# Turning the normalized head results by VectorE's 32x32 blocks and scratch memory instead of by TensorE, in heads 0 to 6 of both kinds

## The reference, cut to what matters

```
def rms_norm(x, g):
    y = xf * lax.rsqrt(jnp.mean(jnp.square(xf), axis=-1, keepdims=True) + RMS_EPS) * g
fo = rms_norm(fo, fox_norm_w_l).reshape(bsz, t_, FOX_WIDTH)      # 8 fox heads
o = rms_norm(o, norm_w) * jax.nn.silu(z)                         # 8 GDN heads
out = jnp.concatenate([fo, go], axis=-1) @ w_out_l               # output projection
```

## Time and profile before

| | us |
|---|---|
| median of 3 runs | 1889.69 (1888.07 to 1890.96) |
| the profiled execution | 1889.48 |
| its span, first to last instruction | 1887.9 |
| granted TensorE clock, mean | 0.997 of full speed |
| fox heads | about 90 to 310 us, one every 30 us |
| GDN heads | about 310 to 700 us, one every 48 us |

### The profile page before, as it was taken

One profiled execution on the slowest core, in us unless ns is written; L12 is line 12 of the kernel. 1 busy time (PEld: TensorE's weight loads), 2 busy tenths in 40 slices (PEclk: granted clock), 3 DMA queues, 4 the chain that ended last, 5 costly groups with the idle time before them and its releaser, 6 DMA issues.

```text
span 1887.9 us, 31205 instructions
## 1 busy us (share of the span) xinstructions
PE 1861.8 (99%) x9409; PEld 1577.3 (84%) x9409; DVE 1076.7 (57%) x2353; ACT 729.3 (39%) x1467; POOL 268.5 (14%) x491
## 2 busy tenths in 40 slices
PE   7999999999999999999999999999999999999997
PEld 6999998888888888888888888888888888888886
DVE  6666666888888874664545454433334444444455
ACT  4444344554555433343333333333333333333330
POOL 2343433333333310001111110000000000000000
PEclk9999999999999999999999999999999999999999
DMA  7666674444444335245556645544445555467441
GB/s 209 184 162 160 164 172 124 117 112 112 116 112 117 117 114 164 91 129 165 156 152 165 173 128 164 162 130 129 129 129 146 145 164 162 122 167 212 162 134 67
DMA packets 317413, 270.77 MB, mean 143 GB/s; under 512 B 96600, under 2 KB 230624, under 8 KB 316704
## 3 DMA queue, kind: packets, MB, share of 16 engines
q1 hardware_dynamic: 306880, 250.90, 47.4%
q0 software_dynamic: 10464, 18.99, 4.0%
HBM read 249.73 MB, written 20.06 MB: 143 GB/s over the span
## 4 chain that ended last, share of the span: by engine, by line
PE 97%; DVE 1%; DMA 1%; SPq 1%; issue 0%; ACT 0%; DVEq 0%; POOL 0%; ACTq 0%; POOLq 0%
PE bank L298 70%; PE bank L2033 9%; PE bank L1769 7%; PE bank L1885 2%; PE bank L1245 1%; PE bank L1227 1%; PE bank L1239 1%; PE bank L1221 1%; SPq L230 1%; DMA x_res<-in_x_sample 0%; PE bank L1195 0%; DMA raw<-in_w_in 0%; PE bank L640 0%; PE bank L1288 0%; PE bank L417 0%
## 5 line engine op out<-in xcount | busy, mean ns | idle before, releaser
L274 DVE TENSOR_TENSOR w_lo<-raw,w_hi 128x512 fp32r<-128x512 f32 (+2 forms) x828 | 565.3, 691 | 620.4 <-ACT w_hi L269 617.2
L269 ACT ACTIVATE w_hi<-raw 128x512 fp32r<-128x512 f32 (+2 forms) x828 | 502.6, 616 | 838.2 <-PE bank L298 700.8
L298 PE MATMUL bank<-w_hi,aT_hi 128*128 128x512 f32 (+2 forms) x1776 | 695.7, 392 | 2.0 <-DVE aT_lo L432 1.6
L298 PE MATMUL bank<-w_hi,aT_lo 128*128 128x512 f32 (+2 forms) x1776 | 673.2, 379 | 0.0
L298 PE MATMUL bank<-w_lo,aT_hi 128*128 128x512 f32 (+2 forms) x1776 | 672.1, 378 | 0.0
L298 PEld LDWEIGHTS bank<-w_hi,aT_hi 128*128 128x128 f32 x1776 | 334.4, 188 | 60.3 <-issue 9.4
L298 PEld LDWEIGHTS bank<-w_hi,aT_lo 128*128 128x128 f32 x1776 | 333.7, 188 | 55.4
L298 PEld LDWEIGHTS bank<-w_lo,aT_hi 128*128 128x128 f32 x1776 | 334.7, 188 | 47.4
L298 PE MATMUL bank<-w_hi,hT_hi 128*128 128x512 f32 x288 | 112.0, 389 | 0.0
L298 PE MATMUL bank<-w_lo,hT_hi 128*128 128x512 f32 x288 | 112.0, 389 | 0.0
L298 PE MATMUL bank<-w_hi,hT_lo 128*128 128x512 f32 x288 | 112.0, 389 | 0.0
(11 more groups left out here) (366 smaller groups left out, 1986.8 us busy)
## 6 DMA issues: line engine op xcount, KB each, us to landing
raw<-in_ffn_w_gate SPq DMA_DIRECT2D x176, 256.0 KB, 2.7
raw<-in_ffn_w_up SPq DMA_DIRECT2D x176, 256.0 KB, 2.7
raw<-in_ffn_w_down SPq DMA_DIRECT2D x176, 256.0 KB, 3.3
raw<-in_w_in SPq DMA_DIRECT2D x128, 192.0 KB, 2.4
raw<-in_w_in SPq DMA_DIRECT2D x128, 128.0 KB, 2.3
raw<-in_w_in SPq DMA_DIRECT2D x256, 64.0 KB, 2.3
raw<-in_w_out SPq DMA_DIRECT2D x61, 256.0 KB, 3.2
h_blocks<-sg SPq DMA_DIRECT2D x11, 768.0 KB, 4.5
```

The source lines that it names most:

```text
L269: nc.scalar.activation(w_hi[:, g % RING, 0:width], raw[:, g % RAW, 0:width], ACT.Copy).then_inc(sem("w_high"), 1)
L274: nc.vector.tensor_tensor(w_lo[:, g % RING, 0:width], raw[:, g % RAW, 0:width], w_hi[:, g % RING, 0:width], ALU.subtract).then_inc(sem("w_ ...
L298: last = nc.tensor.matmul(acc[t][:, 0:width], l[:, k0 + n, t * P:(t + 1) * P], r[:, g % RING, 0:width], start=(n == 0 and j == 0), stop=(n ...
```

## The change

In heads 0 to 6 of both kinds TensorE no longer turns the normalized result. VectorE transposes its 32x32 blocks in one instruction over all three tiles (128x384), to `sc` in fox heads and `R` in GDN heads, and waits for its own last write first. SyncE stores the 192 KB to the scratch tensor `turns`, waits for the store, and loads them back in four DMAs that put the blocks in place, in runs of 32 elements, to `pT` (fox) and `vn` (GDN). ScalarE's high part and VectorE's low part are computed from there in the next head: in fox heads at slot 8 on ScalarE and before the mask additions on VectorE, in GDN heads at slot 14 on both. In the last head of each kind everything stays with TensorE. The results of GDN head h now lie in place h + 1 (mod 8) of `mixG`; head 0 writes place 0 first with values that the last head overwrites.

On SyncE the fox store stands before piece 9 and the load before piece 11; in GDN heads the store stands before piece 11 and the load before piece 14, behind the load of the next states.

```diff
+TURN_STORE_AT, TURN_LOAD_AT, TURN_MIX_AT = 9, 11, 8
...
+            turns = nc.dram_tensor("turns", (TOK, HD), F32, kind="Internal").ap()
+
+            def turned_by_pe(h):
+
+                return isinstance(h, int) and h == HEADS - 1
+
+            def store_turned(sp, tile, ready, count):
+                sp.wait_ge(sem(ready), count)
+                sp.dma_start(turns.rearrange("(t p) f -> p t f", p=P), tile).then_inc(sem("o_stored"), 16)
+
+            def load_moved(sp, tile, h):
+                sp.wait_ge(sem("o_stored"), 16 * (h + 1))
+                for r in range(4):
+                    sp.dma_start(
+                        tile[SQUARE * r:SQUARE * (r + 1), :].rearrange("b (a c) -> b a c", c=SQUARE),
+                        turns.rearrange("(a b) (r c) -> b r a c", b=SQUARE, r=4)[:, r]).then_inc(sem("o_moved"), 16)
...
+                fturn = sc[:].rearrange("p t c -> p (t c)")[:, 0:TOK]
+                fmoved = pT[:].rearrange("p t c -> p (t c)")[:, 0:TOK]
...
-                    yield 41 + min(later, FIRST_TURN_LATER)
-                    W("f_o")
-                    for t in range(TT):
-                        last = nc.tensor.transpose(b3[:, t * P:(t + 1) * P], fo[:, t, :], ident)
-                    last.then_inc(sem("f_oT_ps"), 1)
-                    yield 45 + later
-                    W("f_mix")
+                    if turned_by_pe(h):
+                        yield 41
+                        W("f_o")
+                        for t in range(TT):
+                            last = nc.tensor.transpose(b3[:, t * P:(t + 1) * P], fo[:, t, :], ident)
+                        last.then_inc(sem("f_oT_ps"), 1)
+                        yield 45
+                        W("f_mix")
...
+                    else:
+                        yield TURN_MIX_AT
+                        act.wait_ge(sem("o_moved"), 64 * h)
+                        nc.scalar.activation(mixF_hi[:, bass.ds(h - 1, 1), :], fmoved.unsqueeze(1), ACT.Copy,
+                                             scale=nwf[:]).then_inc(sem("f_mix_hi"), 1)
...
+                        dve.wait_ge(sem("f_mix_hi"), h)
+                        nc.vector.scalar_tensor_tensor(
+                            out=mixF_lo[:, bass.ds(h - 1, 1), :], in0=fmoved.unsqueeze(1), scalar=nwf[:],
+                            in1=mixF_hi[:, bass.ds(h - 1, 1), :], op0=ALU.mult, op1=ALU.subtract)\
+                            .then_inc(sem("f_mix"), 1)
...
+                    if not turned_by_pe(h):
+                        after(last)
+                        nc.vector.transpose(fturn, fo[:].rearrange("p t c -> p (t c)"))\
+                            .then_inc(sem("f_o"), 1)
+                        assert own[0] == F_OWN
+                        return
+                    own[0] += 1
                     last.then_inc(sem("f_o"), 1)
...
+                    def next_turn(n, h):
+                        if n == TURN_STORE_AT:
+                            store_turned(sp, fturn.rearrange("p (t c) -> p t c", t=TT), "f_o", h + 1)
+                        if n == TURN_LOAD_AT:
+                            load_moved(sp, fmoved, h)
                     with sp.Fori(0, HEADS - 2) as i:
                         for n in range(NP_IN):
+                            next_turn(n, i)
                             loads(sp, 2 * NP_IN + n + NP_IN * i, n % RAW, fox_parts(i + 2, n, n % RAW))
...
-                        if p == 2:
-                            W("g_mix")
...
-                    yield LEVELS_DONE + 10
-                    W("g_o")
-                    for t in range(TT):
-                        last = nc.tensor.transpose(tl(turn_bank(h), t), go[:, t, :], ident)
-                    last.then_inc(sem("g_oT_ps"), 1)
+                    if last_head(h):
+                        yield LEVELS_DONE + 10
+                        W("g_o")
+                        for t in range(TT):
+                            last = nc.tensor.transpose(tl(turn_bank(h), t), go[:, t, :], ident)
+                        last.then_inc(sem("g_oT_ps"), 1)
...
+                    yield 14
+                    act.wait_ge(sem("o_moved"), 64 * (HEADS - 1 + h))
+                    nc.scalar.activation(mixG_hi[:, bass.ds(h, 1), :], vn.rearrange("p t c -> p (t c)").unsqueeze(1),
+                                         ACT.Copy, scale=nwg2[:]).then_inc(sem("g_mix_hi"), 1)
...
+                        if n == 1:
+                            W("g_mix_hi")
+                            V.scalar_tensor_tensor(out=mixG_lo[:, bass.ds(h, 1), :],
+                                                   in0=vn.rearrange("p t c -> p (t c)").unsqueeze(1), scalar=nwg2[:],
+                                                   in1=mixG_hi[:, bass.ds(h, 1), :], op0=ALU.mult,
+                                                   op1=ALU.subtract).then_inc(sem("g_mix"), 1)
...
+                    if last_head(h):
+                        own[0] += 1
+                        ins.then_inc(sem("g_o"), 1)
+                    else:
+                        after(ins)
+                        V.transpose(R.rearrange("p t c -> p (t c)"), go[:].rearrange("p t c -> p (t c)"))\
+                            .then_inc(sem("g_o"), 1)
...
+                    if n == STORE_AT - 1:
+                        store_turned(eng, R, "g_o", h + 1)
                     if n == STORE_AT:
                         store_state(eng, h)
                     if n == STORE_AT + 2:
                         eng.wait_ge(sem("g_S_out"), 32 * (h + 1))
                         load_state(eng, h + 1)
+                        load_moved(eng, vn.rearrange("p t c -> p (t c)"), HEADS - 1 + h)
...
-                    dve.sem_inc(sem("g_mix"), 1)
...
-                            last = nc.tensor.matmul(banks[t][:, :], l[:, k % HEADS, t * P:(t + 1) * P], r,
+                            last = nc.tensor.matmul(banks[t][:, :], l[:, k if k < HEADS else (k + 1) % HEADS,
+                                                                      t * P:(t + 1) * P], r,
```

More of the change, by code:

```diff
@@ L104 @@
 SAMPLE_LEVELS = 4
-F_OWN = 14
+F_OWN = 15
 ROWS = 2 * 3 * 8 + 8 * 8
@@ L109 @@
 WARM_IN = 20
-G_OWN = 25
+G_OWN = 26
 G_READ = 15
@@ L898, in fox_act @@
                     nc.scalar.activation(pT[:, 0:4, :], tiles(b6[:, :], 4), ACT.Copy).then_inc(sem("f_pT0"), 1)
-                    yield 41 + min(later, FIRST_TURN_LATER)
-                    W("f_oT_ps")
+                    if not turned_by_pe(h):
+                        return
+                    yield 41
+                    act.wait_ge(sem("f_oT_ps"), 1)
                     nc.scalar.activation(mixF_hi[:, bass.ds(h, 1), :], b3[:, 0:TOK].unsqueeze(1), ACT.Copy, scale=nwf[:])\
@@ L1197, in gdn_pe @@
                     yield 9
-                    L("g_cv", 1, 3), W("g_mix")
+                    L("g_cv", 1, 3)
                     for t in range(TT):
@@ L1387, in gdn_act @@
                     decays(range(5, NB)).then_inc(sem("g_Sdec"), 1)
[L1388 to L1391 removed]
+                    if last_head(h):
+                        yield 48
+                        act.wait_ge(sem("g_oT_ps"), 1)
+                        nc.scalar.activation(mixG_hi[:, bass.ds((h + 1) % HEADS, 1), :], turn_bank(h)[:, 0:TOK].unsqueeze(1),
+                                             ACT.Copy, scale=nwg2[:]).then_inc(sem("g_mix_hi"), 1)
                 def gdn_dve(dve, h):
@@ L1430, in gdn_dve @@
                     dve.wait_ge(sem("g_rows_in"), 16 * (h + 1))
+                    W("g_state")
                     for t in range(TT):
@@ L1550, in gdn_dve @@
                     ins.then_inc(sem("g_state"), 1)
-                    yield 48
-                    W("g_mix_hi")
-                    V.scalar_tensor_tensor(out=mixG_lo[:, bass.ds(h, 1), :], in0=turn_bank(h)[:, 0:TOK].unsqueeze(1),
-                                           scalar=nwg2[:], in1=mixG_hi[:, bass.ds(h, 1), :], op0=ALU.mult,
-                                           op1=ALU.subtract).then_inc(sem("g_mix"), 1)
+                    if last_head(h):
+                        yield 48
+                        dve.wait_ge(sem("g_mix_hi"), h + 2)
+                        V.scalar_tensor_tensor(out=mixG_lo[:, bass.ds((h + 1) % HEADS, 1), :],
+                                               in0=turn_bank(h)[:, 0:TOK].unsqueeze(1), scalar=nwg2[:],
+                                               in1=mixG_hi[:, bass.ds((h + 1) % HEADS, 1), :], op0=ALU.mult,
+                                               op1=ALU.subtract).then_inc(sem("g_mix"), 1)
                     assert own[0] == G_OWN
```

7 lines of the change are left out of this document (2 added, 5 removed).

## The result

The changed kernel takes 1933.74 us (median of four runs, 1928.26 to 1934.76) against 1889.82 for the kernel before beside it: a ratio of 1.0228 (95% interval 1.0215 to 1.0241), 44 us slower. Forecast were 1920 us and the range 1904 to 1934: the median lies 0.3 us inside the upper end, and one of the four executions lies outside. The profiled execution is the lowest of the four, 1928.26 us (span 1926.7).

What follows compares the result with a forecast made beforehand. TensorE, busy 99% of the span, was taken to bound the kernel. Fox +2.5, GDN +24.2 and clock +3.4 gave together +30 on 1889.5: 1919.6, given as 1920 us, range 1904 to 1934.

Steps and rivals of the forecast that it cites:

- a landing at 424 us: GDN blocks: late bound for their last landing, taken as 422.3; it adds 12 us, giving 1932.
- The late blocks: GDN level 1: blocks land behind the state load, ScalarE waits 4.3 us, TensorE stalls 3.15; 22.5 us over seven heads.
- The clock: TensorE's clock: two falls of 1.7 us booked in seven stalls, 3.4 us on.
- rival 1: The clock falls behind every GDN stall: 7 x 1.7 = 12 us in place of 3.4, 1928 us; chance 0.10.
- The low part inside level 1: GDN head 0, blocks already landed: VectorE's 0.55 us meets some 0.4 of room; 0.2 us on.
- The GDN boundary: State additions end later behind the transpose, TensorE waits 0.7 us; the saving becomes 7 x 0.22 = 1.5 us on.
- VectorE's transpose: Fox heads 1 to 6: the awaited split comes 0.60 us later, 3.6 us on; head 0 booked nothing (0 to 0.6).
- The late use: Fox heads 1 to 6: ScalarE waits 3 us for the blocks; 0.2 us a head booked, 1.2 us on.
- The removed transposes: 42 transposes off TensorE: 0.33 us a fox head, 0.50 in six GDN heads, 0.33 in the seventh; 5.6 us off.
- rival 2: GDN blocks land in time, before 418.0, and only VectorE's additions count: 1893.9 us; chance 0.06.
- Rival 3: TensorE's saving shows and the waits have more room than the load times say: 1884 us, faster; chance 0.07.
- Rival 4: SyncE becomes the bound: added issues and the store wait delay weight loads; 1940 us at 1.5 us more; chance 0.09.

Runs made afterwards that it cites:

- e2: Only the fox half of the change, GDN heads as in the kernel before: 1894.48 us, ratio 1.0026.
- e4: The changed kernel with three more unused matmuls per GDN head, issued just before TensorE waits in level 1: 1920.37 us, ratio 1.0160.
- e1: The changed kernel with GDN's four block loads issued ahead of the state stores and the state load: 1898.58 us, ratio 1.0046.
- e5: The changed kernel with GDN's users of the blocks later: ScalarE's high part in slot 24, VectorE's low part ahead of level 5: 1895.44 us, ratio 1.0031.
- e12: e7 with GpSimd's two mask multiplications and the load of the next decay rows moved behind the head's third convolution: 1881.12 us, ratio 0.9960.
- e10: e2 with fox's transpose two weight splits later and its blocks used in slot 15 and behind the maxima: 1886.59 us, ratio 0.9986.
- e11: e7 with three identity transposes by TensorE put back in each head, their result unused: 1888.09 us, ratio 0.9993.
- e6: e5 with VectorE's GDN transpose moved behind the four state additions: 1894.78 us, ratio 1.0025.
- e7: e6 with fox's transpose two weight splits later and its blocks used in slot 15 and behind the maxima: 1887.59 us, ratio 0.9988.

## Why the prediction was right, and where its sizes were off

The direction, the range and the cause hold; the sum was 30 us where 44 came. That the range held is in part luck: its upper end, 1932 to 1934, was worked out from a landing at 424 us and no miss in the clock or the fox heads. The landing came at 422.3, and the excess came from the clock, the fox heads and level 1. The runs give each term:

| term | forecast | measured | from |
|---|---|---|---|
| fox half | +2.5 | +5.0 | e2 - before |
| GDN, blocks late at level 1 | +22.5 | +21.8 | e4 - e1 |
| GDN, the two instructions inside level 1, blocks in time | +0.2 | +3.1 | e1 - e5 |
| GDN boundary, less the saved transposes | +1.5 | +1.0 | e5 - e2 |
| clock | +3.4 | +13.4 | after - e4 |

The last column holds by the way the kernels were built, and the terms share neighbours, so they sum to the whole (44.3) by construction. By the intervals of the ratios each can be off by 2 to 4 us, so the two small GDN terms rest on the traces: from the first to the last first transposes of a GDN head, seven periods, e1 takes 340.8 us, e5 337.8, the kernel before 337.0, which gives 2.9 and 0.8.

**The late blocks: right.** Forecast was a landing behind the state load, a wait of 4.3 us on ScalarE, a stall of 3.15 us; the rows have 4.43 and 3.39, and e4 less e1 gives 21.8 us for seven heads. The landing with the state load in front was the one of two that I took, and e1 shows that place in the queue to be the cause. Put back into the picture of before (the head is 7.74 us later, 414.60 against 406.86), ScalarE goes on at 422.3, as forecast. To the tenth that is luck: the four issues ended about 0.5 us later than booked, and the last block was there 2.3 us behind the end of its issue, where 2.8 were booked.

**The clock: the mechanism was named, the size was wrong.** I booked two falls of 1.7 us in seven stalls. The profiled execution has five, and two of them are twice as long, 11.9 us together; the fill experiment prices the term at 13.4 us. So of rival 1 (12 us) the price was the right one, though not its "behind every stall". My argument against it, that matmuls at full rate stand before and behind a stall, did not help: such matmuls stood around each of the five. The idle time alone was worth more than half as much as the stall that made it.

**The low part inside level 1: booked for head 0 alone.** I set the low part's 0.55 us against 0.4 us of room in head 0. Once the blocks are in time (e1), every head pays: TensorE stands idle 0.47 us before its second product of level 1, behind VectorE's mask and so behind the low part. That took 0.80 us (median) there against 0.61 in e5; GpSimd's multiplication ended at 427.41, in the middle of it, so this is probably the collision of e12 again. Under the stall this cost is hidden behind ScalarE's squares, and the forecast's 22.5 was for the whole of level 1: to be laid beside it is 21.8 + 3.1 = 24.9 by the runs, or about 23.4 by the trace (first to second product of level 1: 1.59 us before, 4.93 after, seven times).

**The GDN boundary: right.** The additions end late by the transpose and TensorE waits 0.81 us (forecast 0.7); with the saved 0.50 the net is about 1 us over seven heads (1.5), which the runs alone could not tell from nothing.

**Fox: the transpose near, the late use too small.** VectorE's transpose was booked at 0.60 in six heads, 3.6 us; it took 0.58, TensorE waited 0.74 (0.16 before), and its price is 4.2 us, head 0 included, where TensorE waits 0.39 at 87.42 and I had booked 0 to 0.6. The late use was the miss, 4.0 us against 1.2. The landing was nearly right (ScalarE goes on at 127.61 with the head 0.23 us later there than before, so 127.4 against 127.1), and the first split behind it found room, as booked; the delay surfaces further on, where I had only guessed "about as much room": the load at 138.03 waits 0.59. Such waits add up to 4.1 us in the kernel after, 1.4 in the mixing of head 1 and 0.4 to 0.6 in each of the next five. The three fox terms (4.2 + 4.0 - 2.3 = 5.9) come to 0.9 more than the fox half's 5.0, which is within what these runs can tell.

**The removed transposes: right in size, and here without effect.** In fox the 0.33 us a head came back in full once nothing stood in front of it (e10, and e11 in reverse). In GDN the 0.50 was eaten: by the boundary in the kernel after, by VectorE held up in e6 and e7; only e12 shows it.

**Rivals 2 to 4.** With everything in time (e5) the kernel takes 1895.44, near rival 2's 1893.9. Rival 3's 1884 is passed by e12, but only with the four users of the blocks, both transposes and GpSimd's multiplication moved. Rival 4 is out: no weight load waited for raw weights.

## What to carry to other kernels

When work is moved off the busiest engine, place its new consumers by the latest landing of their data, not by the earliest free slot: an instruction that waits holds everything queued behind it, and moving two of them by some slots (e5) gave back 38 of 44 us with the late transfer left as it was. Price a stall of TensorE twice where it is as long as here (3.4 us): the time itself, and the clock afterwards. When a saving on one engine does not show, look at whether some instruction of another comes in two lengths; it was there, and not in the list of waits, that the 0.50 us a head had gone.

## What the runs showed of the hardware

VectorE's subtraction of 128x384 from two operands in SBUF took, in e7, 0.56 us in four heads and 1.53 to 1.56 in the other four, where GpSimd's copy and multiplication ran beside it; with the multiplication moved away (e12) it took 0.56 in seven heads of eight. With TensorE's transposes put back (e11) it took 0.56 to 0.73, which is why e11's GDN heads were shorter. The Trainium skill ("SBUF — State Buffer", Who interferes with whom) has the rule: a VectorE instruction with two SBUF inputs and a GpSimd instruction that reads SBUF exclude each other, and the one that starts first keeps the other out for its whole length. The trace agrees: the 0.97 us that the slow subtraction takes more are about GpSimd's copy (0.28) and the first of its two multiplications (some 0.7), and in the quick head of e7, at 416.30, it is the copy beside the subtraction that takes 0.71 us and not 0.28. VectorE's block transpose, with one input, took 0.57 to 0.58 us throughout. So the length of a GpSimd instruction can stand on TensorE's path although GpSimd is busy 14% of the span, and a head 0.5 us quicker on TensorE moved the two into each other.

Four 48 KB loads of 128-byte pieces took SyncE 1.87 us to issue with no large load just before them (e1), and 2.82 and 2.96 right behind a 512 KB load (kernel after, e5); the issue itself is slowed.
